# Dilated attention stage of a two-block transformer kernel: another order of the five projections of a head pair, and attentions dealt out between the products of a projection

## The reference, cut to what matters

```python
hn = rms_norm(h, norm_w)
proj = hn @ w_in                                   # q, k, v for 24 heads, gate g_a for 8 slots
q = rms_norm(q, q_norm_w) * HEAD_DIM ** -0.5;  k = rms_norm(k, k_norm_w)
for c, (window, dilation) in enumerate(((128, 1), (512, 4), (2048, 16))):
    sl = slice(c * N_SLOTS, (c + 1) * N_SLOTS)     # 8 heads of 64 for each dilation
    o_c, lse_c = dilated_window_attention(q[:, :, sl], k[:, :, sl], v[:, :, sl], window, dilation, slopes)
alpha = jax.nn.softmax(jnp.stack(lses, axis=0), axis=0)
o = jnp.sum(alpha[..., None] * jnp.stack(outs, axis=0), axis=0).reshape(B, S, ATTN_WIDTH)
y_a = o * jax.nn.silu(g_a)
```

## Time and profile before

| | us |
|---|---|
| median of three runs (3409.03 to 3409.46) | 3409.13 |
| the profiled execution, its own time | 3411.73 |
| its span | 3409.9 |
| PE busy | 3305.4 (97%) |
| DVE, ACT, POOL busy | 1302.9, 1015.7, 924.9 |

### The profile page before, as it was taken

The page is one execution under the profiler, slowest core; times in us unless marked ns, Lnnn a source line. Parts: engine busy times, 40 slices in busy tenths (PEclk is TensorE's granted clock), DMA queues, the critical chain, the costliest instruction groups (busy, mean ns, idle before and its releaser), DMA issues. The chain is left out here.

```text
span 3409.9 us, 43811 instructions
## 1 busy us (share of the span) xinstructions
PE 3305.4 (97%) x16379; PEld 1810.9 (53%) x16379; DVE 1302.9 (38%) x2804; ACT 1015.7 (30%) x2409; POOL 924.9 (27%) x705
## 2 busy tenths in 40 slices
PE   7999999998999999999999999999999999999999
PEld 4485858584455454444454545454545454545544
DVE  3333434346244244444233323332433242545522
ACT  4314141413334143233233423342434143411100
POOL 1002020205432532632311152115211521161232
PEclk9999999999999999999999999999999999999999
DMA  6101010113120212332071547254634464340321
GB/s 229 32 25 38 21 38 13 33 39 92 31 48 19 51 26 87 119 111 80 22 35 32 40 100 51 32 45 112 37 29 49 108 40 27 61 115 13 142 93 62
DMA packets 282365, 202.43 MB, mean 59 GB/s; under 512 B 124380, under 2 KB 249708, under 8 KB 278528
## 3 DMA queue, kind: packets, MB, share of 16 engines
q1 hardware_dynamic: 279052, 199.62, 31.1%
q10 hardware_dynamic: 3104, 0.01, 0.1%
HBM read 153.79 MB, written 45.81 MB: 59 GB/s over the span
## 5 line engine op out<-in xcount | busy, mean ns | idle before, releaser
L2465 PE MATMUL d<-hT,roll 128*128 128x512 f32 x1280 | 579.4, 596 | 2.1 <-PEq L76 2.1
L2465 PE MATMUL d<-w_room,roll 128*128 128x512 f32 x960 | 433.8, 594 | 0.0
L2465 PEld LDWEIGHTS d<-hT,roll 128*128 128x128 f32 x1280 | 242.4, 191 | 300.8 <-issue 299.3
L600 PE MATMUL m<-hT,roll 128*128 128x512 f32 x704 | 321.1, 593 | 1.3 <-ACT pre L750 1.3
L2465 PEld LDWEIGHTS d<-w_room,roll 128*128 128x128 f32 x960 | 180.6, 190 | 220.8 <-issue 219.1
L2502 POOL TENSOR_TENSOR w_z<-w_u,w_y 128x512 f32<-128x512 f32 x40 | 50.7, 1267 | 788.1 <-ACT w_y L2471 775.5
L1412 PE MATMUL n<-hT,roll 128*128 128x512 f32 x512 | 226.8, 598 | 1.8 <-PEq L76 1.8
L600 PEld LDWEIGHTS m<-hT,roll 128*128 128x128 f32 x704 | 124.9, 191 | 116.0 <-issue 115.8
L1412 PE MATMUL n<-mix_na,roll 128*128 128x512 f32 x384 | 169.4, 594 | 1.3 <-POOL roll L1312 1.3
L548 POOL TENSOR_TENSOR hn<-hn 128x512 f32<-128x512 f32 x16 | 17.5, 1093 | 545.6 <-DVE hn L917 545.6
L3126 ACT ACTIVATE mix_f<-sneg,negmax 128x192 f32<-128x192 f32 (+1 forms) x384 | 160.7, 423 | 5.5 <-DVE negmax L3240 3.6
(11 more groups left out here) (403 smaller groups left out, 5253.5 us busy)
## 6 DMA issues: line engine op xcount, KB each, us to landing
roll<-in_w_in SPq DMA_DIRECT2D x128, 256.0 KB, 3.0
mix_f<-alpha SPq DMA_DIRECT2D x48, 192.0 KB, 6.3
xg<-in_x SPq DMA_DIRECT2D x4, 2048.0 KB, 16.9
roll<-in_w_in SPq DMA_DIRECT2D x16, 512.0 KB, 3.9
rb<-r_rows SPq DMA_DIRECT2D x16, 512.0 KB, 4.9
mix_ml<-in_x SPq DMA_DIRECT2D x16, 512.0 KB, 3.4
x<-mix_ml SPq DMA_DIRECT2D x16, 512.0 KB, 3.0
o_rows<-mix_f SPq DMA_DIRECT2D x8, 1024.0 KB
```

The costliest lines, as they stand in the source:

```text
L600: last = nc.tensor.matmul(bank[n % 2][:], w[:, k], hT[:, k, (n % 4) * TB:(n % 4 + 1) * TB], start=(k == 0), stop=(k == KC - 1))
L2465: last = nc.tensor.matmul(bank[self.bank_of(n, j, i)][:], w[:, k], x[k], start=(k == 0), stop=(k == h - 1))
```

## The change

- The projections of a pair stand in another order: p=0 makes the values of dilations 16 and 1, p=1 keys and queries of dilation 4, p=2 its values and the gate, p=3 keys and queries of dilation 1, p=4 those of dilation 16. The attentions are those of dilation 4, 1 and 16. The values made in p=0 are parked in DRAM (`v_rows`, `w_rows`).
- An attention is cut in slots (`attend`). After each product of the next projection one slot is issued: the attention of dilation 4 runs in p=3, that of dilation 1 in p=4, that of dilation 16 in p=0 of the next pair. The very last one has no projection beside it.
- The products use two PSUM banks instead of four, and the scores two instead of four.
- The pieces of the combination stand in p=1 and p=2 instead of p=0 and p=1.
- The row statistics of all three dilations are stored by `store_stats`; the transposed way is gone.

```diff
-    a, b = ((k0 + H, q0 + H), (v0 + H, v0), (k0 + 2 * H, q0 + 2 * H), (v0 + 2 * H, g0), (k0, q0))[p]
+    a, b = ((v0 + 2 * H, v0), (k0 + H, q0 + H), (v0 + H, g0), (k0, q0), (k0 + 2 * H, q0 + 2 * H))[p]
...
-    BANKS = 4
+    FIRST_BANK, BANKS = 2, 2
...
-        if i == 1:
-            need(pe, self.held, 2 * s)
-        elif i == 5:
-            pe.wait_ge(self.held, 2 * s + 1)
+        if i in (3, 6):
+            pe.wait_ge(self.held, 2 * s + {3: 1, 6: 2}[i])
         else:
-            need(pe, self.full, 5 * s + {2: -2, 3: -1, 4: 0, 6: 1, 7: 2}[i])
+            need(pe, self.full, 5 * s + {1: -1, 2: 0, 4: 1, 5: 2, 7: 3}[i])
...
-        return (1, 2, 0)[a % N_CFG]
+        return (1, 0, 2)[a % N_CFG]
...
+    def first_turn(a):
+        return 4 if cfg(a) == 2 else 2
...
+                    if g > 0:
+                        store_stats(a - 1)
+                    load(n + 1, 2)
+                    store_x(n, 1, w_dst)
+                    store_y(n, 1, v_dst)
+                    load(n + 1, 3)
...
+                    load(n + 4, 1)
                     store_stats(a)
+                    load(n + 4, 0, 2)
+                    sp.wait_ge(y_kept, 16 * (4 * g + 2))
+                    sp.wait_ge(z_kept, 16 * (4 * g + 2))
+                    fetch_values(a + 1, v_dst)
                     store_rows(a)
                     load(n + 4, 3)
 
                     load(n + 5, 1)
                     store_stats(a + 1)
+                    load(n + 5, 0, 2)
+                    sp.wait_ge(x_kept, 16 * 2 * (g + 1))
+                    sp.wait_ge(u_kept, 16 * 2 * (g + 1))
+                    fetch_values(a + 2, w_dst)
                     store_rows(a + 1)
+                    load(n + 5, 3)
+                store_stats(NA - 1)
...
+                def attend(a, slot):
+
                     if a < 0:
                         return
+                    if slot == 1:
+                        if cfg(a) != 1:
+                            sums(a, 7)
+                        turn_values(a, 0)
+                        turn_values(a, 1)
+                    elif slot == 2:
+                        turn_values(a, 2)
+                        turn_values(a, 3)
+                    k = slot - first_turn(a)
+                    if 0 <= k < NB:
+                        turns(a, k)
+                    if (-2 if cfg(a) == 2 else 0) <= k < NB - 2:
+                        scores(a, k + 2)
+                    if 0 < k <= NB:
+                        values(a, k - 1)
...
+                for slot in range(1, NB + 5):
+                    attend(NA - 1, slot)
```

More of the change, by code:

```diff
@@ new lines, in project_keys @@
+                    hold(n, 0, 1)
+                    for slot in (1, 2, 3):
+                        attend(b, slot)
+                    hold(n, 0, 4)
+                    square(a, 0)
+                    if g > 0 and cfg(a) == 1:
+                        late.factors_act(nc, act, g - 1)
+                    for slot in (4, 5):
+                        attend(b, slot)
+                    root(a, 0)
+                    square(a, 1)
+                    for slot in (6, 7):
+                        attend(b, slot)
@@ L3204, in _ @@
                 for a in range(NA):
+                    if cfg(a) == 1:
+                        project_first_values(a)
                     project_keys(a)
[L3206 removed]
+                    if cfg(a) == 1:
                         project_values(a)
[L3208 to L3211 removed]
+                for slot in range(1, NB + 4):
+                    attend(NA - 1, slot)
             @block.vector
@@ L3267, in write_out, with start, attend @@
                     nc.vector.tensor_copy(dst, src).then_inc(out, 1)
-                def tail(a, step):
+                def start(a, k):
+                    if k == 0:
+                        if a % N_CFG == 0:
+                            dve.wait_ge(bias_in, 48 * (a // N_CFG + 1))
+                        if a >= N_CFG:
+                            dve.wait_ge(late.st_stored, 16 * stat_stores(a - 1))
+                    for i in range(BU):
+                        biased_min(a, k, i)
+                def attend(a, slot):
@@ L3270, in tail @@
                     if a < 0:
                         return
-                    if step < 2:
-                        copies(a, NB - 2 + step)
-                    write_out(a, NB - 3 + step)
+                    if slot == 1 and cfg(a) != 1:
+                        norm(a, 7)
+                    if slot == 2:
+                        for m in range(2, 4):
+                            dve.wait_ge(v_turned, 4 * a + m + 1)
+                            if a % N_CFG == 0 and m == 2:
+                                need(dve, late.mixed, late.PIECES * (a // N_CFG))
+                            nc.vector.tensor_copy(vals[:, 4 * m:4 * m + 4], bank[T_BANK + m][:, :].rearrange("p (c l) -> p c l", l=P)).then_inc(v_dve, 1)
@@ new lines, in attend, with project_first_values @@
+                    k = slot - first_turn(a)
+                    if 2 <= k <= NB + 1:
+                        write_out(a, k - 2)
+                    if 0 <= k < NB:
+                        copies(a, k)
+                    if (-2 if cfg(a) == 2 else 0) <= k < NB - 2:
+                        start(a, k + 2)
+                def project_first_values(a):
+                    n = 5 * (a // N_CFG)
+                    for j in range(2):
+                        for i in range(1, 8):
+                            if i not in (1, 4):
+                                add(n, j, i)
+                            attend(a - 1, 7 * j + i)
@@ new lines, in project_keys @@
+                    weighing = g > 0 and cfg(a) == 1
+                    attend(b, 1)
+                    add(n, 0, 2)
+                    attend(b, 2)
+                    add(n, 0, 3)
+                    attend(b, 3)
+                    if weighing:
+                        late.lower_dve(nc, dve, g - 1)
+                    attend(b, 4)
+                    add(n, 0, 5)
+                    attend(b, 5)
+                    if weighing:
+                        late.invert_dve(nc, dve, g - 1)
@@ L3342, in _ @@
                 for a in range(NA):
+                    if cfg(a) == 1:
+                        project_first_values(a)
                     project_keys(a)
-                    if cfg(a):
+                    if cfg(a) == 1:
                         project_values(a)
-                    attend(a)
-                tail(NA - 1, 0)
-                tail(NA - 1, 1)
-                tail(NA - 1, 2)
+                for slot in range(1, NB + 6):
+                    attend(NA - 1, slot)
         clear(nc, sems, sems[0])
@@ L4014 @@
     "v_rows": (PAIRS, P, T),
+    "w_rows": (PAIRS, P, T),
     "g_rows": (PAIRS, P, T),
```

464 lines of the change are left out of this document (206 added, 258 removed).

## The result

The changed kernel takes 3574.2 us (median of 4 runs, 3570.7 to 3582.6), the kernel before beside it 3409.1: 1.049 times as long, 95% interval 1.047 to 1.051. Forecast were 3580 and 3520 to 3630. The sum came out; two of its terms did not, in opposite directions, and the profile shows which.

The account below looks back on a forecast made before the run. PE, busy 97% of the span, was taken as the bound. 3411.7 - 17.4 (gaps, switches, transposes) + 140 (weights) + 25 (clock) + 23 (end) = 3582.3; the runs' median lies 2.6 lower: 3580 us, range 3520 to 3630.

Parts of the forecast that it names:

- Switches: PE alternating products and attention pieces: 91 more switches at 0.10 us, +9.1; eight transposes of the statistics dropped, -1.0.
- Gaps closed: PE's 29.1 us idle in the dilated stage all go, except 3.6 us in the last attention: net -25.5.
- The weights: Quarter 3 queues behind statistics stores (S: first store issue); ten PE waits, 49 + 40 + 51: +140 us, bounds 90 to 180.
- The first rival: Quarter 3 of the weights arrives in time, as transfers pass each other or the queue drains faster: 3415 us, chance 0.10.
- The clock: PE at half clock after each of ten waits for weights, 2.5 us each: +25; another 2.5 counted at the stage's end.
- The end: Last statistics store: next stage starts 14.5 us late, its combination chain waits 6 more, clock 2.5: +23 (14 to 30).
- The rival on the faster side: Quarter 3 in time and the last store hidden, SP issuing eight DMAs in under 5 us: 3392 to 3395, chance 0.07.
- The forecast's own case: Whole kernel: quarters of weights wait behind the statistics in SP's queue, 3580 us, 5% slower, range 3520 to 3630, chance 0.74.

Follow-up runs that it names:

- the later run: The changed kernel, unaltered, run again in the last batch on another chip than the first two experiment batches: 3548.8 us, ratio 1.041 to the kernel before.

## Why the prediction came out, and what was wrong in it

**The sum.** By the profiles: forecast -25.5 for gaps, +8.1 for switches and the dropped transposes, +140 for weights, +27.5 for the clock (its 2.5 at the end included), +20.5 for the end: 170.6. Measured: +27.0 (55.2 - 28.2), +6.6 (PE's busy time with row-by-row statistics), +83.7, +32.4, +23.0 (26.7 - 3.7): 172.7, where the span grew by 170.9. Two errors of 52 and 56 us cancelled. That the total came within 6 us of the forecast is luck.

**Switches.** The 6.6 us are not their price, near as they are to 8.1. The windows view of the whole stage, from its first product to that of the next stage, in the kernel before, with rows of statistics, and with these and DVE's order:

```profile
1612.40:2962.10 1349.70, 1320.48 (x7168) 673.71 (x7168) 466.18 (x1277) 468.62 (x1272) 339.14 (x305) 1.00 0.46 51
1609.70:2992.30 1382.60, 1328.19 (x7161) 675.86 (x7161) 451.86 (x1278) 471.48 (x1268) 340.04 (x306) 0.99 0.19 56
1613.90:2947.00 1333.10, 1320.40 (x7160) 673.38 (x7160) 460.20 (x1277) 469.94 (x1268) 340.70 (x305) 0.99 0.21 58
```

With the same switches PE is busy 7.7 us longer than before in the second row and not at all in the third. What goes with DVE's order is half clock: in the second kernel it is granted behind each of the four waits of 3.4 us for negmax, for instance 0.50 from 1849.5 to 1852.9. Together with the transposes that went, the switches cost nothing that these rows show; +8.1 was a term too many.

**Gaps closed, the step that failed most.** "With a product of 3.4 us between two blocks, ACT and DVE have over 5 us for a block that now takes them 2 to 3. I let all 29.1 us go, except in the last attention". I compared amounts of work and not DVE's order: the copy of the one bank of values stood behind an addition that itself waits for the product, and with two banks the second scores wait for the first's minimum, which stood behind two norms. That is shown: with the order changed the other waits of the stage fall by 42.7 us, and nothing else in the program is different. Even with that edit the term is -14.7 (13.5 - 28.2) and not -25.5: half of what is left are sums that wait for ACT, 7.2 us, which I had not seen coming either.

**The weights.** Between p=0 and p=1 I had 51 us, and 52.8 came (16.0, 20.4, 16.4). That is in part luck: PE arrives at S + 25.1 for 22.7, and the mix is ready at S + 41.1, 45.4 and 41.5 for 39.8, both later than forecast; in the later run the three waits are 44.4. Between p=4 and p=0 40, and 21.5 came; between p=3 and p=4 49, and 4.2. Two things were mis-sized. Landings: S + 48.4, 43.3, 41.7 and 47.0 in p=3, 49.5, 47.2 and 49.0 in p=4, for 51.3. And PE arrived later, at S + 46.4 the first time instead of 40.4, because of 5.8 us of waits, nearly all of the kind just named, which I had put at zero; with DVE's order changed it was there at S + 40.2. The mechanism also was half right. "So the queue serves in order, and a quarter pays for all that stands ahead": it pays on ACT's queue too, for elements that do not stand ahead of it there. For the place in one queue the sentence holds in its direction, but 1 MB less ahead of quarter 3 brought 2.5 us and not 7.4. The first rival, that quarter 3 is there in time, is refuted by the changed kernel itself: landings from S + 41.7 and 83.7 us of waits. So is what I drew from the Trainium skill ("DMA: Bandwidth & Descriptors", Queues, rings and completion order) for that rival: completion out of order may be so, and on a second queue the quarters did pass elements, but it freed no quarter in time here.

**The clock.** The term was 27.5 us for ten waits and the end, and 32.4 came, for eleven waits of 0.75 to 20.4 and the end; with the 6.6 behind the waits that DVE's order made it is 39.0, all that PE is busy longer.

**The end.** The barrier's wait, 14.5 us, was met (14.46), but with luck: SP issued for 16.6 us and not 19.2, while the 14.46 include the barrier's own wait, 1.2 us in the kernel before, so 13.3 are new. The chain behind it grew by 9.7 us (12.2 - 2.5) instead of 6. The rival on the faster side, an issue in under 5 us, was false, by the same 16.6 us.

**Chances.** The forecast's own case happened only in part, and the 3549 us of the later batch show how much of the range the elements' own spread takes.

## What to carry to other kernels

Before moving a store next to loads that are waited for, count its packets and not its bytes: 32 KB in packets of 4 bytes made a load of 256 KB that was issued with them or right behind them take 16 to 29 us instead of 3.0, even on another queue, and a permutation of columns that costs nothing left one packet of every 4 or 16. When work is interleaved, compare on each engine the order of its instructions and what each waits for, not only the sum of their durations: one copy behind a waiting addition cost PE 29 gaps, 26.9 us in all. When variants differ by less than two runs of one kernel do, compare landings and arrivals before the times. And when a total comes out, check the terms.

## What the runs showed of the hardware

- In the two runs of the changed kernel eight DMAs with 8192 packets of 4 bytes keep SP issuing for 13.6 to 22.0 us, and the first quarter behind them lands 31.1 to 42.9 us after their first issue. With the loads on ACT's queue SP issues for up to 30.4 us, and a quarter issued 3 to 8 us after S lands at S + 20.9 to 33.7. 2048 packets of 16 bytes occupy SP for 5.3 us, and the quarter behind them lands 5.0 us after its issue. Timeline of SP in the kernel with the columns:

```profile
1809.21 2.67 SPq L2775 DMA_DIRECT2D stats<-negmax  x4
1811.92 2.60 SPq L2775 DMA_DIRECT2D stats<-total  x4
```

- A second issuing engine gives room for issuing (the wait at the barrier, 13.0 and 14.5 us in the changed kernel, becomes 7.6), but no faster transfers here.
- The same program took 3574 us in one batch and 3549 in another, while the kernel before took 3409 and 3407. What makes the elements slower in one of them, the chip or the run, stays open.
